# Second block's attention scores: one f32 matmul for each head, or three rounded products from parted keys and queries

## The reference

```python
# layer 0 of the second block
def dilated_mixture_attention(q, k, v):      # 8 heads, kind "a"
    q = q * (dh ** -0.5)                     # three window patterns, softmax over all of them
def differential_attention(q1, q2, k1, k2, v, lam, lam_init, subln_g):   # 4 heads, kind "b"
    def attn(q, k):
        s = einsum('bhqd,bhkd->bhqk', qs, k) * scale + bias
        return softmax(s, axis=-1)
    a = attn(q1, k1) - lam * attn(q2, k2)
    return einsum('bhqk,bhkd->bhqd', a, v32)
# layer 1: 16 query heads on 4 key heads, a band of 128 positions on each side, kind "c"
s = einsum('bgrnid,bgncd->bgrnic', qb, kw)
s = s - slopes * dist
y = acc * e / (l * e + exp(sk - M))
```

## Time and profile before

| | us |
|---|---|
| median of 3 runs | 2685.91 |
| lowest and highest | 2684.38, 2688.58 |
| the profiled execution, its own time | 2686.96 |
| its span in the trace | 2685.2 |
| PE busy (share of the span) | 2484.5 (93%) |
| DVE, ACT, POOL busy | 968.2, 900.5, 834.6 |

### The profile page before, as it was taken

The page is one execution under the profiler, slowest core; times in us unless marked ns, Lnnn a source line. Parts: engine busy times, 40 slices in busy tenths (PEclk is TensorE's granted clock), DMA queues, the critical chain, the costliest instruction groups (busy, mean ns, idle before and its releaser), DMA issues.

```text
span 2685.2 us, 36074 instructions
## 1 busy us (share of the span) xinstructions
PE 2484.5 (93%) x14117; PEld 2034.8 (76%) x14117; DVE 968.2 (36%) x1599; ACT 900.5 (34%) x1368; POOL 834.6 (31%) x503
## 2 busy tenths in 40 slices
PE   6989989968999999998999998999998999889997
PEld 3866877867888888887887566888787886677766
DVE  3663565043322223333213224222343004731173
ACT  4423333322322222233321234333333225623362
POOL 1453264213322222233241003444344441024302
PEclk8988989989999999998887998999998999988999
DMA  6248138311122121211210001233232221112211
GB/s 268 78 188 315 63 134 311 133 32 55 48 62 62 62 62 56 64 60 50 75 55 16 1 1 63 87 100 94 86 89 103 95 96 65 49 55 78 78 47 63
DMA packets 56946, 234.84 MB, mean 87 GB/s; under 512 B 6336, under 2 KB 7616, under 8 KB 56064
## 3 DMA queue, kind: packets, MB, share of 16 engines
q1 hardware_dynamic: 56592, 232.44, 25.5%
q0 software_dynamic: 240, 0.79, 0.1%
HBM read 231.11 MB, written 2.10 MB: 87 GB/s over the span
## 4 chain that ended last, share of the span: by engine, by line
PE 77%; DVE 5%; ACT 2%; issue 2%; POOL 0%; DMA 0%; DVEq 0%; ACTq 0%; POOLq 0%
PE ps L733 15%; PE ps L734 15%; PE ps L735 15%; PE ps L1310 4%; PE ps L1312 4%; PE ps L1313 4%; PE ps L574 2%; PE ps L1405 2%; PE ps L1403 1%; PE ps L1486 1%; PE ps L1499 1%; PE ps L1422 1%; PE ps L771 1%; PE ps L770 1%; PE ps L772 1%
## 5 line engine op out<-in xcount | busy, mean ns | idle before, releaser
L432 POOL TENSOR_TENSOR w_low<-ring,w_high 128x1024 fp32r<-128x1024 f32 (+2 forms) x267 | 624.3, 2339 | 1624.9 <-ACT w_high L425 1624.9
L425 ACT ACTIVATE w_high<-ring 128x1024 fp32r<-128x1024 f32 (+2 forms) x267 | 274.8, 1032 | 1034.4 <-PE ps L735 690.9
L733 PE MATMUL ps<-h_high,w_high 128*128 128x512 f32 x1104 | 437.5, 396 | 12.4 <-DVE h_low L675 11.6
L734 PE MATMUL ps<-h_low,w_high 128*128 128x512 f32 x1104 | 434.9, 394 | 0.0
L735 PE MATMUL ps<-h_high,w_low 128*128 128x512 f32 x1104 | 433.8, 393 | 0.0
L733 PEld LDWEIGHTS ps<-h_high,w_high 128*128 128x128 f32 x1104 | 210.5, 191 | 59.5 <-issue 12.3
L735 PEld LDWEIGHTS ps<-h_high,w_low 128*128 128x128 f32 x1104 | 210.1, 190 | 44.8
L734 PEld LDWEIGHTS ps<-h_low,w_high 128*128 128x128 f32 x1104 | 210.8, 191 | 41.4
L1310 PE MATMUL ps<-hidden,w_high 128*128 128x512 f32 (+1 forms) x528 | 190.2, 360 | 14.6 <-issue 14.6
L1312 PE MATMUL ps<-hidden,w_high 128*128 128x512 f32 (+1 forms) x528 | 189.8, 360 | 0.0
L1313 PE MATMUL ps<-hidden,w_low 128*128 128x512 f32 (+1 forms) x528 | 189.4, 359 | 0.0
(11 more groups left out here) (350 smaller groups left out, 4815.9 us busy)
## 6 DMA issues: line engine op xcount, KB each, us to landing
XB<-ada_dram SPq DMA_DIRECT2D x84, 768.0 KB, 6.1
ring<-up_dram SPq DMA_DIRECT2D x88, 512.0 KB, 3.6
ring<-down_dram SPq DMA_DIRECT2D x44, 512.0 KB, 3.6
ring<-winE_dram SPq DMA_DIRECT2D x32, 512.0 KB, 3.3
ring<-win_dram SPq DMA_DIRECT2D x20, 512.0 KB, 3.6
ring<-winC_dram SPq DMA_DIRECT2D x20, 512.0 KB, 3.2
arena<-ada_dram SPq DMA_DIRECT2D x12, 768.0 KB, 20.8
XB<-xl_dram SPq DMA_DIRECT2D x2, 2048.0 KB, 9.2
```

The lines of the kernel that those rows point to most:

```text
L425: nc.scalar.activation(WH[p][:, 0:L], RAW[p][:, 0:L], ACT.Copy).then_inc(w_hi, 1)
L432: nc.gpsimd.tensor_tensor(WL[p][:, 0:L], RAW[p][:, 0:L], WH[p][:, 0:L].bitcast(F32), ALU.subtract)\
L733: nc.tensor.matmul(bank[:, 0:n], wh[:, cols], hi, start=(k == 0), stop=False)
L734: nc.tensor.matmul(bank[:, 0:n], wh[:, cols], lo, start=False, stop=False)
```

## The change

The scores of a, b and c are no longer one f32 matmul for each head and unit but three rounded ones that add up in the same bank: high part of the queries with high part of the keys, low with high, high with low. For that, the queries and keys of a pair are parted first: ACT copies the 128x512 tile in f32 to the rounded type (the high part), POOL subtracts it from the tile (the low part). That is done pair by pair. The parts lie in places that are free in this stage: queries in `squares_rounded` (four tiles), keys in `key_parts` (four tiles), so two pairs at a time. In c a tile of keys serves four pairs, so c parts 2 tiles of keys and 8 of queries; a and b part 4 and 4 each. All in all 26 copies on ACT and 26 subtractions on POOL.

Where they run: pairs 0 and 1 of a in the middle of `winE` on ACT; each later pair at the head of the first unit of the pair before it; pair 0 of b at the head of a's last pair. Pairs 0 and 1 of c come after the last sum of `winC` is taken and before ACT rounds the first two chunks of `woutC`. POOL does its subtractions in the same sequence right behind the last weight chunk of `winE` or `winC`, so ahead of the first chunks of `woutE` or `woutC`. PE waits for the low part of a pair's queries at the first unit of the pair.

```diff
+        E_KR = parts("key_parts", H_AT + KT * S, 4, S)
...
+        E_PARTED = [(what, kind, p) for kind in "abc" for p in range(PAIRS[kind]) for what in "kq"
+                    if kind != "c" or what == "q" or p % 4 == 0]
...
                 def scores(u):
                     p, i = divmod(u, 4)
                     kts = key_tiles(kind, i)
                     a, b = kts[0] * P, (kts[-1] + 1) * P
+                    if i == 0:
+                        pe.wait_ge(e_lo, E_PARTED.index(("q", kind, p)) + 1)
+                    _, qh, ql = e_parts("q", kind, p)
+                    _, kh, kl = e_parts("k", kind, p)
                     for x in range(2):
-                        bank = open_bank(pe, kind + "S", 2 * u + x)
-                        o = 64 * x
-                        ins = nc.tensor.matmul(bank[:, 0:b - a], Q[o:o + 64, p, i * P:(i + 1) * P],
-                                               K[o:o + 64, p // own, a:b], start=True, stop=True)
-                        sums_done(ins, kind + "S", 2 * u + x)
+                        to = open_bank(pe, kind + "S", 2 * u + x)[:, 0:b - a]
+                        o, at = slice(64 * x, 64 * x + 64), slice(i * P, (i + 1) * P)
+                        MM = nc.tensor.matmul
+                        MM(to, qh[o, at], kh[o, a:b], start=True, stop=False)
+                        MM(to, ql[o, at], kh[o, a:b], start=False, stop=False)
+                        sums_done(MM(to, qh[o, at], kl[o, a:b], start=False, stop=True), kind + "S", 2 * u + x)
...
+            def part_pair(kind, p):
+
+                for what, _, _ in [x for x in E_PARTED if x[1:] == (kind, p)]:
+                    before_ = earlier(kind, 4 * p, 5)
+                    if before_ and (p >= 2 or kind == "b"):
+                        await_sums(act, before_[0] + "S", 2 * before_[1] + 1)
+                    await_taken(act, *e_source(what, kind, p))
+                    whole, high, _ = e_parts(what, kind, p)
+                    A(high, whole, ACT.Copy).then_inc(e_hi, 1)
...
                 for u in range(n + 2):
+                    if u % 4 == 0 and u < n:
+                        p = u // 4 + 1
+                        if p < PAIRS[kind] and (p >= 2 or kind == "b"):
+                            part_pair(kind, p)
+                        elif p == PAIRS[kind] and kind == "a":
+                            part_pair("b", 0)
...
                     taken(A(C_G[:, g - 12, :], bank[:, :], ACT.Silu), "winC", g)
+            for p in range(2):
+                part_pair("c", p)
             split_hi("woutC", 0)
...
+                if stage in ("winE", "winC"):
+                    for x, (what, kind, p) in enumerate(E_PARTED):
+                        if (kind == "c") == (stage == "winC"):
+                            whole, high, low_ = e_parts(what, kind, p)
+                            pool.wait_ge(e_hi, x + 1)
+                            TT(low_, whole, high.bitcast(F32), ALU.subtract).then_inc(e_lo, 1)
```

More of the change, by code:

```diff
@@ L965, in two_blocks, with e_parts, e_source @@
         lam_sem = sem("lam_sem")
+        e_hi, e_lo = sem("e_hi"), sem("e_lo")
+        E_PARTED = [(what, kind, p) for kind in "abc" for p in range(PAIRS[kind]) for what in "kq"
+                    if kind != "c" or what == "q" or p % 4 == 0]
+        def e_parts(what, kind, p):
+            pp = PAIRS_BEFORE[kind] + p
+            Q, K = dict(a=(E_QA, E_KA), b=(E_QB, E_KB), c=(C_Q, C_K))[kind]
+            if what == "q":
+                return Q[:, p, :], SQR[:, 2 * (pp % 2), :], SQR[:, 2 * (pp % 2) + 1, :]
+            k = p // 4 if kind == "c" else p
+            return K[:, k, :], E_KR[:, 2 * (k % 2), :], E_KR[:, 2 * (k % 2) + 1, :]
+        def e_source(what, kind, p):
+            if kind == "c":
+                return ("winC", p if what == "q" else 8 + p // 4)
+            return ("winE", (12 if kind == "b" else 0) + (4 if what == "k" else 0) + p)
         def key_tiles(kind, i):
@@ L1462, in attention @@
                 n = 4 * PAIRS[kind]
-                Q, K, VT = dict(a=(E_QA, E_KA, E_VA), b=(E_QB, E_KB, E_VB), c=(C_Q, C_K, C_V))[kind]
+                VT = dict(a=E_VA, b=E_VB, c=C_V)[kind]
                 own = 4 if kind == "c" else 1
@@ L1872, in _ @@
                     taken(A(dst[g][0], bank[:, :], ACT.Copy, scale=dst[g][1]), "winE", g)
+                if g == 14:
+                    for p in range(2):
+                        part_pair("a", p)
             split_hi("woutE", 0)
```

## The result

The changed kernel takes 2688.63 us (median of 20 runs, 2680.49 to 2697.05), the kernel before 2684.19 in the same session (20 runs). The ratio, estimated from all these runs, is 1.0026, with a 95% interval of 1.0016 to 1.0035: **slower, by some 7 us** (4.3 to 9.4); the two medians alone lie 4.4 us apart. The forecast was 2.9 us faster.

A forecast was written before the change was run, and what follows sets the result against it. PE was taken to bound a and c, and to be coupled with DVE in b. Terms of -2.2 (a), -1.2 (b), -1.5 (c) and +2.0 (c's start) gave -2.9 us: median 2683.0 us, range 2678 to 2698.

## What to carry to other kernels

Work put on an idle engine is free only if it touches nothing that a busy engine holds: before giving GpSimd a subtraction, look at which VectorE operations with two inputs in SBUF stand on the path at that time, and put it where there are none. A product made shorter just ahead of a wait can cost the clock more than it gains; read the granted clock of the stretch behind each wait, and keep TensorE at work there or shorten the wait. Trace the kernel before twice, and compare stages with the clock beside them: a change of 0.2% can't be taken apart by total times.

## What was not expected of the hardware

- While GpSimd subtracts from SBUF, VectorE's operations with two inputs in SBUF wait for its end: over all traces 0.22 becomes 0.64 to 1.11 us, 0.75 becomes 1.72 to 2.80, and 0.16 becomes 1.09 for eight elements. Those that read PSUM don't (0.68 as ever), nor does one with a single input in SBUF (0.15).
- A wait of TensorE of 1.83 us behind products of 1.81, 1.72 and 1.93 busy of 2 us each was followed by 3.4 us at 1.2 GHz, one of 1.68 us behind 1.97, 1.93 and 1.95 was not. At b's start the kernel before has the same wait of 1.22 us in both of its traces, and a fall behind it in one of them only.
- Matmuls on the two halves of the rows overlap in the same way whether three of one head or one of each are issued first: 0.90 to 0.91 us for the shortest units.
